# VectorE's order in the last phase of a two-layer kernel: one row addition after each unit's low parts, instead of two after each pair of units

## The reference, cut to what matters

```python
def chunk(args):
    xc, ec, gc = args                                   # 128 tokens, their 128 chosen experts, the gates
    a = jnp.einsum('cd,ckd->ck', xc, expert_u[ec])      # dots with the rows of u
    w = (gc * jax.nn.gelu(a.astype(jnp.float32))).astype(x.dtype)
    return jnp.einsum('ck,ckd->cd', w, expert_v[ec])    # weighted sum of rows of v
```

## Time and profile before

| what | value |
|---|---|
| median of 3 runs | 2427.22 us (2425.97 to 2429.71) |
| the profiled execution's own time | 2426.9 us |
| its span | 2424.9 us |
| TensorE matmul busy | 2382.4 us, 98% of the span |
| VectorE busy | 1724.2 us, 71% |
| ScalarE busy | 836.3 us, 34% |
| GpSimd busy | 1150.3 us, 47% |
| granted TensorE clock, mean | 0.997 |
| first to last matmul of the v phase (line 1295) | 1884.9 to 2418.7 us |

### The profile page before, as it was taken

One profiled execution on the slowest core, in us unless ns is written; L12 is line 12 of the kernel. 1 busy time (PEld: TensorE's weight loads), 2 busy tenths in 40 slices (PEclk: granted clock), 3 DMA queues, 4 the chain that ended last, 5 costly groups with the idle time before them and its releaser, 6 DMA issues.

```text
span 2424.9 us, 35086 instructions
## 1 busy us (share of the span) xinstructions
PE 2382.4 (98%) x12248; PEld 2030.8 (84%) x12248; DVE 1724.2 (71%) x2873; ACT 836.3 (34%) x1445; POOL 1150.3 (47%) x747
## 2 busy tenths in 40 slices
PE   8999999999999999899999999999999999999999
PEld 6888888888888887666889999999999888888887
DVE  8888785462433556776628699799887788788777
ACT  4132222100113324776224333444443333333333
POOL 6777776666665550203563788721122333333321
PEclk9999999999999999899999999999999999999999
DMA  4333323333332223000224899999999999999995
GB/s 149 99 108 105 104 95 128 131 108 117 133 108 92 87 80 122 27 1 10 70 87 136 294 309 304 309 347 345 347 338 408 369 342 352 343 347 350 344 345 199
DMA packets 181333, 490.41 MB, mean 202 GB/s; under 512 B 14848, under 2 KB 80512, under 8 KB 181248
## 3 DMA queue, kind: packets, MB, share of 16 engines
q1 hardware_dynamic: 144384, 355.12, 43.8%
q0 software_dynamic: 36864, 134.23, 14.6%
HBM read 436.86 MB, written 52.43 MB: 202 GB/s over the span
## 4 chain that ended last, share of the span: by engine, by line
PE 89%; issue 3%; POOL 3%; DVE 2%; ACT 1%; DMA 1%; SPq 0%; POOLq 0%; ACTq 0%; DVEq 0%
PE ps L689 39%; PE ps L1295 22%; PE ps L1255 17%; POOL spl L2658 2%; PE ps L1276 2%; PE ps L1134 2%; PE ps L1108 1%; POOL rare L2668 1%; PE ps L873 1%; PE ps L1047 1%; PE ps L993 1%; PE ps L1093 0%; DVE st L2218 0%; PE ps L794 0%; PE ps L893 0%
## 5 line engine op out<-in xcount | busy, mean ns | idle before, releaser
L1255 PE MATMUL ps<-hh,spl 128*128 128x384 f32 x2048 | 535.5, 337 | 2.8 <-POOL spl L2658 2.8
L689 PE MATMUL ps<-hh,spl 128*128 128x512 f32 x1728 | 535.2, 389 | 1.5 <-DVE x L1934 0.8
L1295 PE MATMUL ps<-spl,wsp 128*128 128x512 f32 x2304 | 533.2, 391 | 0.1
L1295 PEld LDWEIGHTS ps<-spl,wsp 128*128 128x128 f32 x2304 | 428.1, 188 | 102.7 <-DVE wsp L2484 13.3
L1647 ACT ACTIVATE spl<-ring 128x1024 fp32r<-128x1024 f32 x256 | 271.6, 1061 | 691.3 <-PE ps L1255 344.8
L2531 POOL TENSOR_TENSOR spl<-ring,spl 128x1024 fp32r<-128x1024 f32 (+1 forms) x164 | 428.4, 2612 | 13.1
L689 PEld LDWEIGHTS ps<-hh,spl 128*128 128x128 f32 x1728 | 324.4, 188 | 69.5 <-DVE x L1934 1.2
L1255 PEld LDWEIGHTS ps<-hh,spl 128*128 128x128 f32 x2048 | 370.9, 188 | 6.1 <-issue 5.3
L2529 POOL CAST spl<-ring 128x1024 fp32r<-128x1024 f32 (+1 forms) x164 | 185.1, 1129 | 355.6 <-PE ps L689 336.1
L1255 PE MATMUL ps<-hl,spl 128*128 128x384 f32 x1024 | 342.5, 334 | 0.0
L2429 DVE TENSOR_TENSOR spl<-ring,spl 128x1024 fp32r<-128x1024 f32 x192 | 234.7, 1222 | 148.5 <-ACT spl L1647 148.2
(11 more groups left out here) (451 smaller groups left out, 3403.3 us busy)
## 6 DMA issues: line engine op xcount, KB each, us to landing
ring<-stream_in SPq DMA_DIRECT2D x134, 512.0 KB, 3.5
ring<-u_in SPq DMA_DIRECT2D x128, 512.0 KB, 5.3
ring<-v_in SPq DMA_DIRECT2D x128, 512.0 KB, 6.2
ring<-stream_in SPq DMA_DIRECT2D x60, 704.0 KB, 4.1
gelu<-gst SPq DMA_DIRECT2D x128, 192.0 KB, 5.7
dense<-stage SPq DMA_DIRECT2D x12, 2048.0 KB, 13.1
gl<-gelu SPq DMA_DIRECT2D x32, 768.0 KB, 6.8
gw<-dense SPq DMA_DIRECT2D x32, 768.0 KB, 9.3
```

The costliest lines, as they stand in the source:

```text
L689: m = pe.matmul(ps[:, bank, :], w[:, part, k0 + k * n:k0 + k * n + P], rhs(k), start=first and k == 0 and part == 0 and rhs is high, stop= ...
L1255: m = pe.matmul(ps[:, bank, 0:TD], w[:, part, k0 + k * P:k0 + (k + 1) * P], rhs(k), start=first and k == 0 and part == 0 and rhs is high, ...
L1295: m = pe.matmul(ps[:, bank, :], wsp[:, j % 2, part, tok], spl[:, j % 2, row, cols], start=False, stop=last and n == 2)
```

## The change

In each pair of units VectorE's order was: low parts of unit 2p, low parts of unit 2p+1, `weigh`, addition 2p, addition 2p+1. It becomes: low parts of unit 2p, addition 2p, low parts of unit 2p+1, `weigh`, addition 2p+1. No instruction is added or removed; addition 2p moves ahead of the low parts of unit 2p+1.

```diff
@@ -2496,10 +2496,9 @@
                 for k in (2 * p, 2 * p + 1):
                     weight_low(N_KEYS + k, i, 16)
                     low(i, k)
-                if to_weigh is not None:
-                    weigh(*to_weigh)
-                for s in range(2 * p, 2 * p + 2):
-                    add_row(i, s)
+                    if k % 2 and to_weigh is not None:
+                        weigh(*to_weigh)
+                    add_row(i, k)
```

## The result

| | before | after |
|---|---|---|
| median, 5 runs each | 2426.0 us (2425.0 to 2429.71) | 2415.12 us (2414.73 to 2415.63) |
| profiled execution: own time, span | 2426.9, 2424.9 us | 2415.56, 2413.6 us |
| mean granted clock | 0.997 | 0.997 |

The ratio is 0.995 with a 95% interval of 0.994 to 0.9961: faster by 10.9 us in the medians, where 9.3 were forecast.

A forecast was written before the change was run, and what follows sets the result against it. TensorE, 98% busy, was taken as the bound, held up in the v phase by VectorE's loop. Removing 9.3 us there takes the profiled 2426.9 to 2417.6, plus 0.3 for the median: 2417.9 us, range 2415.0 to 2422.5.

The forecast's parts named there:

- the term for what follows the last load: From the v phase's last load (2418.68) to the span's end (2424.9): taken as unchanged, with no gain counted.
- the sum: Steady v-phase loads: 2289 take 518.9 us at the 0.2267 pitch instead of 528.19, a gain of 9.3 us.
- The bound and the loop: v phase: TensorE waits on a loop closed by VectorE, 16.68 us per four units where TensorE alone needs 16.32.
- One sign: Among the signs that would show the forecast right: nothing before 1883, ahead of the v phase's steady run, has moved.
- The odd unit's cover: Low part, low and addition before the odd unit take 2.81 us, under 4.08; VectorE's idle time there covers it.
- The additions' own wait: An addition's 0.2 us wait for the one before, 56 times, 11.3 us in all, goes; counted at nothing.
- The queues behind an addition: Gathers and SyncE's loads behind the moved addition keep enough cover: some 24 us for gathers; v loads move under a microsecond.
- the range's lower end: 2415.0 us, where all 11.8 us of listed idle time and a little of the runs' spread come back.
- Rivals 1 and 2: VectorE's low parts wait for a running gather, of 0.94 us (2423.3 us) or 1.67 us (2446.7 us); chance 0.05 each.
- Rival 3: Transfers already set the v phase's pace at 346 GB/s, so no change: 2427.2 us; chance 0.05.
- rival 4: Half of the v phase's loss comes from something else, waits shifting rather than ending: 2422.6 us; chance 0.05.

## Why the prediction was right, and where it was short

In short: the mechanism in the loop was right and sized within 0.2 us. The step that failed is the term for what follows the last load, which the sum held fixed at 6.2 us and which became 4.9.

**The bound and the loop: right.** The waits of line 1295 on line 2484 are gone, four units take 16.31 us (16.32 worked out), the steady run 518.72 us (518.9), and VectorE idles 0.32 and 1.19 us ahead of even and odd units (0.4 and 1.2). One sign did not hold: something before 1883 did move, by 0.5 us. The limit of the loop, 4.81 or 4.82 us for VectorE's step, was not only argued: steps of 4.3 us cost nothing, 4.87 a little, 5.41 the most.

**The odd unit's cover: right.** The addition in front of the odd unit lies in idle time, and 1.19 us of it are left.

**The additions' own wait: its share was not seen.** The prediction counted it at nothing beside the stall that it was a part of. The sum was not hurt, since that stall was counted whole; but before the change this wait was on the path, and with weigh between the additions its going was alone worth 8.0 of the 9.5 us. The loop was over its limit by 0.35 us, and the wait was 0.30 of it.

**The end of the kernel: the step that failed.** The sum ended at the last load of the v phase (2418.68) and took what came behind it, 6.2 us, as fixed. "The queues behind an addition" went through the gathers, the loads and the quads of SyncE's queue, and left out its stores. The last addition releases the rare tile's stores, and with the old order these came so late that SyncE's eight issues, 4.47 us in one piece, ended 1.9 us behind ScalarE's last copy. Moving one addition out of the way took 1.3 us off. That is the term that was missing, with 0.2 in the loop beside it; the remaining 0.5 of the 11.3 us between the two profiles lies ahead of the v phase. The forecast of 2417.9 us was 2.8 over the median measured, with the whole gain sized at 9.3 in place of 10.9. Of these 2.8 us 2.0 are the three terms just named (1.3, 0.2 and 0.5); 0.3 had been added for the median of the runs before, and the median after lies 0.4 under its own profiled execution; both are spread between runs. That 2415.12 still lies above the range's lower end of 2415.0 is in part luck: that end stood for a loop that gives back up to 11.8 us, and the loop gave 9.5. The rest came from the end, which the prediction did not have, and from ahead of the v phase.

**The rivals.** Rivals 1 and 2, a gather that holds VectorE, are refuted by the trace of the changed kernel. GpSimd's timeline, which answers to the earlier trace rows:

```profile
2001.50 0.94 POOL L2676 DMA_INDIRECT rare<-v_in,rstd  x1 [2.27 <-DVE ps L2491]
2006.45 0.94 POOL L2676 DMA_INDIRECT rare<-v_in,rstd  x1 [4.01 <-DVE ps L2491]
2009.66 0.94 POOL L2676 DMA_INDIRECT rare<-v_in,rstd  x1 [2.27 <-DVE ps L2491]
```

The gather of 2006.45 runs to 2007.39, and the even low part starts inside it at 2006.50, 1.10 us after ScalarE's high part of 2005.40 started, the ordinary step. It is so all through: between 1903.73 and 2353.03, 110 of the 118 low parts of units started while a gather was being issued, and all 118 started 1.09 or 1.10 us after ScalarE. By the Trainium skill's rule ("SBUF — State Buffer", "Who interferes with whom"), as the prediction read it, the one of 2006.50 would have waited until 2007.39; this trace does not agree. What is lengthened is a gather that starts behind a low part: the one of 2292.29, 0.19 us behind, took 1.85 us. Rival 3, the transfers, falls with the 354 GB/s; rival 4, half of the loss from something else, with the pitch of 0.2266.

## What to carry to other kernels

When a helper engine with much idle time makes the bound engine wait, follow the loop from the bound engine's release through every helper and back, and compare its length with what the bound engine needs for the same number of units: the difference, here 0.35 us in 16.3, is the whole prize of the loop, and any reordering that takes that much out of the loop gets it, not only the obvious one. Here an addition that waited for the one before it cost 0.3 us, which an independent instruction between the two hid. Follow each moved instruction to the last queue it releases, the final stores too.

## What the runs showed of the hardware that was not expected

The part ahead of the v phase is the same code in all these kernels, yet its end moved by some 4 us from profile to profile: the first load of line 1295 started at 1884.33 in the changed kernel, at 1888.12 in the first profile with both additions in the even unit. The granted clock of one place in the first layer explains it. Windows of 10 us, of the changed kernel and then of that other one (the clock is the third number from the end):

```profile
830.00:840.00 10.00, 10.00 (x58) 8.64 (x57) 3.30 (x11) 1.38 (x3) 3.41 (x2) 1.00 0.18 52
840.00:850.00 10.00, 10.00 (x50) 8.01 (x49) 5.11 (x7) 2.37 (x4) 5.11 (x4) 1.00 0.26 76
```
```profile
830.00:840.00 10.00, 10.00 (x48) 8.58 (x47) 3.79 (x11) 1.38 (x3) 3.39 (x2) 0.75 0.17 52
840.00:850.00 10.00, 10.00 (x44) 7.95 (x43) 3.61 (x4) 1.18 (x2) 3.43 (x2) 0.91 0.18 54
```

In the second the mean clock falls to 0.75 and 0.91, so for part of the time the lower of the two levels, 1.2 in place of 2.4 GHz, was granted: 0.25 x 10 + 0.09 x 10 = 3.4 us of the 3.8. Windows of 1 us of the second place the fall in 835 to 836, and the return in 841 to 842:

```profile
834.00:835.00 1.00, 1.00 (x11) 1.00 (x11) 0.00 (x0) 0.31 (x1) 0.92 (x2) 1.00 0.76 152
835.00:836.00 1.00, 1.00 (x7) 1.00 (x7) 0.00 (x0) 0.00 (x0) 1.00 (x1) 0.52 0.90 356
842.00:843.00 1.00, 1.00 (x6) 0.84 (x5) 0.00 (x0) 0.00 (x0) 0.00 (x0) 1.00 0.00 0
```

What TensorE did just before the fall is 24 matmuls with a single column each, here in the timeline of the second:

```profile
832.93 1.84 PE L884 MATMUL ps<-cst,sqs 128*128 128x1 f32 x16
834.63 1.48 PE L873 MATMUL ps<-cst,sqs 128*128 128x1 f32 x8
```

The changed kernel has the same run there (from 832.44) and keeps its clock. Of the eleven profiles of this case four show a fall at this place (0.75 here and 0.83 in three others, over 830 to 840), and their steady runs start at 1891.98 to 1893.79; in the seven without it they start at 1889.67 to 1890.72. So the same code keeps its clock in one execution and loses it for some microseconds in another. That these small matmuls are the cause was not tested. The spread is more than the 0.6 us by which two orders of the end differ, so such differences are to be read from the steady run and the end, not from the total.
